# Stage passages of a two-block transformer kernel, taken tile by tile of the tokens

## The reference, cut to what matters

```python
x = x + 0.5 * g1 * swiglu(modulate(x, sh1, sc1), gate, up, down)   # FFN 1
x = x + g2 * token_mix(modulate(x, sh2, sc2), ...)                 # mix
x = x + 0.5 * g3 * swiglu(modulate(x, sh3, sc3), gate, up, down)   # FFN 2
# modulate(x, shift, scale) = rms_norm(x) * (1 + scale) + shift
# shift, scale, gate come from silu(c) @ w_ada + b_ada, for each stage anew
# swiglu(u) = (silu(u @ gate) * (u @ up)) @ down
# after two layers: x = rms_norm(x) * final_norm, then
# h = modulate_2(x, ...) enters the hybrid layer, h2 = modulate_2(x, ...) the experts
```

## Time and profile before

| | us |
|---|---|
| median of 3 runs (1957.5 to 1962.37) | 1959.36 |
| the profiled execution | 1957.13 |
| its span | 1955.5 |
| PE busy | 1812.3 (93%) |
| DVE busy | 1375.6 (70%) |
| ACT busy | 953.6 (49%) |
| DMA, mean over the span | 224 GB/s |
| chain that ended last | PE 77%, DVE 14%, ACT 4%, DMA 3%, issue 3% |
| mean granted TensorE clock | 0.956 |

### The profile page before, as it was taken

How to read it: one execution, slowest core, us unless ns; L and a number is a source line. 1 busy time by engine, 2 the same in 40 slices (tenths; PEclk the granted TensorE clock), 3 DMA queues, 4 the chain that set the end, 5 groups by cost and what they waited for, 6 DMA issues and landing times.

```text
span 1955.5 us, 25172 instructions
## 1 busy us (share of the span) xinstructions
PE 1812.3 (93%) x8756; PEld 1462.4 (75%) x8772; DVE 1375.6 (70%) x2086; ACT 953.6 (49%) x1427; POOL 47.1 (2%) x92
## 2 busy tenths in 40 slices
PE   6799999999999998999999989998997997999996
PEld 3688777777688767886878767886886675788875
DVE  6877755766766568776567567665677276999886
ACT  4344453654444443444446553444443245777774
POOL 0000000000000000000000000000000000000000
PEclk8899998999999999999989999999998598999998
DMA  9988741224766648884413347664685051999992
GB/s 368 348 307 306 281 144 65 108 92 150 259 252 246 248 174 322 321 306 174 144 65 108 108 173 290 243 244 178 232 326 217 0 193 67 354 352 368 352 352 112
DMA packets 61497, 437.41 MB, mean 224 GB/s; under 512 B 6768, under 2 KB 7280, under 8 KB 9200
## 3 DMA queue, kind: packets, MB, share of 16 engines
q1 hardware_dynamic: 47200, 339.27, 46.6%
q0 software_dynamic: 12672, 92.28, 12.8%
q10 hardware_dynamic: 1552, 4.89, 0.7%
HBM read 435.36 MB, written 1.05 MB: 223 GB/s over the span
## 4 chain that ended last, share of the span: by engine, by line
PE 77%; DVE 14%; ACT 4%; DMA 3%; issue 3%; POOL 0%; ACTq 0%; DVEq 0%; SPq 0%; POOLq 0%
PE bank L1609 22%; PE bank L1610 22%; PE bank L1611 22%; DVE w_lo L886 3%; DMA ada_w<-ada_pairs 2%; DVE ada_w L910 2%; PE bank L1819 2%; PE bank L1836 1%; PE bank L1689 1%; ACT w_hi L485 1%; PE bank L1797 1%; PE bank L1793 1%; PE bank L1799 1%; DVE arena L972 1%; DVE w_lo L893 1%
## 5 line engine op out<-in xcount | busy, mean ns | idle before, releaser
L886 DVE TENSOR_TENSOR w_lo<-raw,w_hi 128x1024 fp32r<-128x1024 f32 x428 | 504.0, 1221 | 258.1 <-ACT w_hi L485 257.1
L485 ACT ACTIVATE w_hi<-raw 128x1024 fp32r<-128x1024 f32 x428 | 428.7, 1053 | 419.1 <-PE bank L1611 413.9
L1609 PE MATMUL bank<-w_hi,uT_hi 128*128 128x512 f32 (+3 forms) x1440 | 561.2, 390 | 22.7 <-DVE uT_lo L1173 11.5
L1610 PE MATMUL bank<-w_lo,uT_hi 128*128 128x512 f32 (+3 forms) x1440 | 547.7, 380 | 0.0
L1611 PE MATMUL bank<-w_hi,uT_lo 128*128 128x512 f32 (+3 forms) x1440 | 546.1, 379 | 0.0
L1609 PEld LDWEIGHTS bank<-w_hi,uT_hi 128*128 128x128 f32 x1440 | 274.4, 191 | 81.6 <-DVE uT_lo L1173 13.5
L1609 PE MATMUL bank<-w_hi,r_arena 128*128 128x512 f32 (+1 forms) x744 | 301.8, 406 | 13.5 <-DVE r_arena L958 5.7
L1611 PEld LDWEIGHTS bank<-w_hi,uT_lo 128*128 128x128 f32 x1440 | 274.2, 190 | 52.0
L1610 PEld LDWEIGHTS bank<-w_lo,uT_hi 128*128 128x128 f32 x1440 | 274.9, 191 | 48.4 <-issue 1.4
L1611 PE MATMUL bank<-w_hi,r_arena 128*128 128x512 f32 (+1 forms) x744 | 297.6, 400 | 0.0
L1610 PE MATMUL bank<-w_lo,r_arena 128*128 128x512 f32 (+1 forms) x744 | 297.6, 400 | 0.0
(11 more groups left out here) (316 smaller groups left out, 1522.7 us busy)
## 6 DMA issues: line engine op xcount, KB each, us to landing
raw<-weight_stream SPq DMA_DIRECT2D x216, 1024.0 KB, 4.9
ada_w<-ada_pairs POOLq DMA_DIRECT2D x88, 1024.0 KB, 5.2
raw<-expert_blocks SPq DMA_DIRECT2D x48, 1024.0 KB, 4.8
ada_w<-expert_blocks SPq DMA_DIRECT2D x32, 1024.0 KB, 4.8
cmpw<-expert_blocks SPq DMA_DIRECT2D x16, 1024.0 KB, 4.8
arena<-ada_pairs SPq DMA_DIRECT2D x5, 1024.0 KB, 13.7
ada_w<-ada_pairs SPq DMA_DIRECT2D x3, 1024.0 KB, 13.2
cmpw<-compress_w ACTq DMA_DIRECT2D x2, 1024.0 KB, 8.3
```

The costliest lines, as they stand in the source:

```text
L485: act.activation(w_hi[:, b], v, ACT.Copy).then_inc(hi_done, 1)
L886: V.tensor_tensor(w_lo[:, b], v, f32(w_hi[:, b]), ALU.subtract).then_inc(split_done, 1)
L1609: pe.matmul(dst, xh, w_hi[:, off:off + n], start=first, stop=False, skip_group_check=True)
L1610: pe.matmul(dst, xh, w_lo[:, off:off + n], start=False, stop=False, skip_group_check=True)
```

## The change

In the code after, a passage is called `arrive` on each engine. x is updated in half rows (`update`), each followed by its own square on ACT (`square`), and the sum of two halves is made on DVE (`total`); ACT takes 1/D and EPS into the root. The normed row is made half on DVE and half on ACT. A tile is turned, scaled, rounded and subtracted in two halves of four k. Tile 1's updates stand between tile 0's steps in DVE's list. PE starts the next stage's first products with tile 0 and turns tile 1 at k = 6. The zero products before the turn are 10 in place of 16. The last FFN unit goes by tile: gate/up of tile 0, the gate product, `down` of the unit before, gate/up of tile 1 with the turn of tile 0 in its middle, then `last_down` by tile and half. The second unit's gate/up of tile 0 goes ahead of the first unit's turn. The first gate pair stands behind all splits of the first unit. On entry to FFN 2 the two rows of c are loaded behind the whole passage. The attention gates' products go in between tile 1's products of the mix. `LAST_UNIT` puts the last unit's third block ahead of the next stage's first.

```diff
-LAST_UNIT = (-1, 0, 3)
+LAST_UNIT = (-1, 0, 2)
 # ACT
-                norm(l * 3 + 2, l * 3 + 2, late=u_mix + MIX_IN_UNITS + MERGE_UNITS, c_row=l)
+            def arrive(q, n, blocks=lambda i: None):
+                square(q, 0)
+                normed(q, 0)
+                blocks(0)
+                act.wait_ge(mod_ready, n + 4)
+                turned(n, 0, 0)
+                blocks(1)
+                square(q, 1)
+                turned(n, 0, 1)
+                normed(q, 1)
+                for h in range(2):
+                    turned(n, 1, h)
...
+                arrive(l * 3 + 2, l * 3 + 2, lambda i: split(u_ffn, (i,)))
+                act.dma_start(c_bc, c_rows[0]).then_inc(c_landed, 16)
+                act.dma_start(c_next, c_rows[l]).then_inc(c_landed, 16)
+                act.wait_ge(c_landed, l * 32 + 48)
+                act.activation(c_bc, c_bc, ACT.Silu).then_inc(c_ready, 1)
+                act.activation(c_next, c_next, ACT.Silu).then_inc(c_ready, 1)
 # DVE
+            def arrive(stage, q, n, blocks=lambda i: None):
+                update(stage, 0, 0)
+                update(stage, 0, 1)
+                blocks(0)
+                total(q, 0)
+                normed(q, 0)
+                blocks(1)
+                dve.wait_ge(mod_ready, n + 4)
+                turned(n, 0, 0)
+                update(stage, 1, 0)
+                rest(n, 0, 0)
+                blocks(2)
+                turned(n, 0, 1)
+                update(stage, 1, 1)
+                rest(n, 0, 1)
+                total(q, 1)
+                normed(q, 1)
+                for h in range(2):
+                    turned(n, 1, h)
+                    rest(n, 1, h)
 # DVE, first unit of ffn2 (ffn1 alike, without the wait)
-                split(u0 + 1, (0,), LAST_BEHIND)
+                first_unit(u0, f0, stage)   # hidden 0, split, hidden 1, split, split
                 dve.wait_ge(c_ready, l * 2 + 3)
                 ada_pair(pair_place(l, "gate2", 0), mods_gate[:, 0:2])
-                hidden(f0)
-                split(u0 + 1, (1,), LAST_BEHIND)
-                split(u0, (2,), LAST_BEHIND)
                 h_split(f0)
 # PE
+            def arriving(n, q, more=lambda k, t: None):
+                def beside(k, t):
+                    if (k, t) == (0, 0):
+                        pe.wait_ge(x_ready, ...)      # tile 1's first half
+                    if (k, t) == (6, 0):
+                        turn_x(n, q, 1)
+                    if k % 4 == 0:
+                        pe.wait_ge(uT_ready, 4 * n + 2 * t + k // 4 + 1)
+                    more(k, t)
+                return beside
+            def arrive(n, q):
+                keep_warm(10, GU[0][:, :])
+                turn_x(n, q, 0)
...
+                pe.wait_ge(h_done, 2 * f0 + 1)
+                gate_up(u0 + 1, TILE[0])
+                turn(f0)
+                gate_up(u0 + 1, TILE[1])
```

More of the change, by code:

```diff
@@ L478, in _, with split @@
         def _(act):
-            def split(u, js, order=IN_LINE):
+            def split(u, js, order=IN_LINE, halves_=range(HALVES)):
                 for j in js:
@@ L508, in norm @@
[L508 to L529, removed]
@@ L533, in gate_out, with silu, h_tile @@
                 act.activation(gate_bc[:, h * 512:(h + 1) * 512], b[:, :], ACT.Copy).then_inc(gate_ready, 1)
[L535 to L539, removed]
+            def silu(u, f, tiles=range(T)):
+                for t in tiles:
+                    act.wait_ge(*((gu0_done, f + 1), (used[1], u + 2))[t])
+                    act.activation(act_g[:, t], GU[t][:, 0:F_UNIT], ACT.Silu).then_inc(silu_done, 1)
+            def h_tile(f, t, psum, done):
+                s = slice(t * P, (t + 1) * P)
+                act.wait_ge(*psum)
+                act.activation(hT_hi[:, :, s], HT[:, :].rearrange("p (f s) -> p f s", f=2)[:, :, s], ACT.Copy).then_inc(done, 1)
             def h_split(f):
@@ L951, in hidden, with turned, rest @@
-            def hidden(f):
-                for t in range(T):
+            def turned(n, t, h):
+                s = slice(t * P, (t + 1) * P)
+                dve.wait_ge(uT_psum, 4 * n + 2 * t + 2)
+                for i in range(2):
+                    c = 4 * h + 2 + i
+                    e = V.tensor_scalar(uTf[:, c, s], turned_banks(n)[t][1][:, (2 * h + i) * P:(2 * h + i + 1) * P], modf[:, 8 + c:9 + c], modf[:, c:c + 1], ALU.mult, ALU.add)
+                e.then_inc(uTf_done_v, 1)
+            def rest(n, t, h):
+                s = slice(t * P, (t + 1) * P)
+                dve.wait_ge(uT_hi_done, 4 * n + 2 * t + h + 1)
+                V.tensor_tensor(uT_lo[:, 4 * h:4 * h + 4, s], uTf[:, 4 * h:4 * h + 4, s], f32(uT_hi[:, 4 * h:4 * h + 4, s]),
+                                ALU.subtract).then_inc(uT_ready, 1)
@@ L1000, in ffn1 @@
                     h_split(f0 + i)
-                split(u0 + n, (0,), LAST_BEHIND)
+                for j in range(2):
+                    ada_pair(pair_place(l, "end1", j), mods[:, 36 + 2 * j:38 + 2 * j])
                 dve.wait_ge(mods_kept, l * 17 + 10)
@@ L1044, in ffn2, with merge @@
                     h_split(f0 + i)
-                split(u0 + n, (0,), LAST_BEHIND)
                 dve.wait_ge(mods_kept, l * 17 + 18)
                 modulation(stage + 1, mods[:, 40:56], gain=vec[:, bass.ds(V_GAIN + l * 8, 8)])
-                split(u0 + n - 1, (2,), LAST_UNIT)
-                hidden(f0 + n - 1)
-                h_split(f0 + n - 1)
-                split(u0 + n, (1,))
-                x_update(stage, (used[2], u0 + n + 1))
-            def merge(u0, m, stage, gates, following, between, more=True):
+                last_unit(u0, f0 + n - 1, n)
+            def merge(u0, m, gates, following):
                 split(u0, (2,))
@@ L1081, in merge @@
                 split(u0 + 2, (2,))
-                x_update(stage, (used[1], u0 + 4), between=between)
-                if more:
-                    split(u0 + 3, (0,))
             def job_bias(j0, jobs, j):
@@ L1725, in ffn @@
-                turn(f0 + n - 1)
-                down(u0 + n - 1, f0 + n - 1, last=True)
+                turn(f - 1)
+                gate_up(u0 + n - 1, TILE[0])
+                pe.wait_ge(gate_ready, 2 * nn + 1)
+                gate(nn, 1, SPARE)
+                down(u0 + n - 2, f - 1)
+                gate_up(u0 + n - 1, TILE[1], beside=lambda k, t: turn_tile(f, 0, hL_psum) if k == KD // 2 else None)
+                last_down(u0 + n - 1, f)
             def half_product(lhs, chunks, closes, ready, done, late=lambda: None):
```

446 lines of the change are left out of this document (260 added, 186 removed).

## The result

| | before | after |
|---|---|---|
| median us (4 runs each) | 1958.43 | 1995.84 |
| lowest to highest | 1955.44 to 1962.37 | 1992.45 to 1999.15 |
| the profiled execution | 1957.13 | 1992.45 |
| its span | 1955.5 | 1990.8 |
| mean granted TensorE clock | 0.956 | 0.939 |

The account below looks back on a forecast made before the run. PE, busy 93%, with its gaps bounded by a DVE, ACT, PE, DVE chain, DVE's list and pair loads. The terms, mainly +14.6 (mix to FFN 2) and +6.4 (experts' entry), summed to +24.5 us on 1957.13, hence 1982; range 1957 to 1994.

Parts of the forecast that it names:

- steps 1, 3, 5: FFN 1 to mix (+1.4, +1.0 us), FFN 2 to FFN 1 (-1.2), FFN 2 to the hybrid layer (-3.2).
- E: Time mark: the start of a stage's last gate/up product.
- step 3: FFN 2 to FFN 1: gate/up ends earlier, but PE waits for the pair chain at the second turn; -1.2 us.
- step 6: Hybrid merge to the experts: tile 1's update waits for tile 0's turn, gate copy later; +6.4 us, bounds +3 to +8.
- Step 2: Mix to FFN 2, twice: late c rows and DVE's list delay the second turn; +7.3 us each, +14.6.
- The real price is in DVE's list: Mix to FFN 2: the first gate pair, behind DVE's three splits, makes the second turn +5.5 us later.
- L: Time mark: the end of a merge's last product.
- a later wait takes such a loss in: Half-pace losses after new waits in mix to FFN 2, FFN 2 to FFN 1, first FFN 1: absorbed, no term.
- The clock: Half-rate products behind waits: +2.6 us in FFN 1 to mix and the hybrid entry, +1.8 per mix to FFN 2.
- A: Faster: DVE's list does not decide, second unit's hidden ready when PE ends down; 1943 us, chance 0.13.
- B: No change: waits at k = 4 mostly absent, experts' entry costs 3, pair chain 4 us sooner; 1960 us, chance 0.09.
- C: Worse: passages restart at 1.2 GHz at k = 4 and tile 1, c's rows land after 7.0 us; 1992, chance 0.14.

Follow-up runs that it names:

- x6: Kernel after, at the experts' entry only: tile 1's half updates on DVE and squares on ACT moved ahead of tile 0's scaling; 1987.45 us, ratio 1.0145.
- b2: Kernel before, with only the first gate pair of each FFN moved behind all splits of the first unit in DVE's list; 1959.48 us, ratio 1.0012.
- x5: Kernel after, with the four pairs of each FFN's own gate no longer all ahead of the second unit's hidden in DVE's list; 1962.75 us, ratio 1.0033.
- b1: Kernel before, with only the four gate pairs of each FFN spread over units 1 to 3 behind the hidden tiles; 1949.02 us, ratio 0.9945.
- w1: Kernel after, with zero products in the waits of passages, first units, second turns and mixes; 1984.30 us, ratio 1.0139.
- x4: Kernel after, with tile 1's squares moved behind the scaling and rounding of tile 0's second half in ACT's list; 1977.21 us, ratio 1.0107.
- w2: Kernel before, with zero products ahead of FFN turns, the hybrid layer's norms and in the mixes' waits; 1950.71 us, ratio 0.9960.
- y3: A faster kernel with zeros in the passages and reordered loops, plus 8 more zero products in each of two mix waits; 1910.96 us, ratio 0.9769.

## Why the prediction was right in sign and wrong in size

- **The passages themselves** (steps 1, 3, 5): right, order and times, to 0.2 us at four points of FFN 1 to mix; FFN 2 to FFN 1 reached gate/up's end at E+28.7 (28.4), the hybrid layer's first block ended at E+40.3 (39.1). But the waits of 2.8 and 2.0 us at k = 4 were 1.06 and 0.28: the places were right while part of the waits was filled by slow products.
- **Given back at the second turn** (step 3): right. Up to there FFN 2 to FFN 1 was 6.4 us ahead, and this wait took 4.8 back (it was 6.19). PE after:

```profile
757.44 1.11 PE L1798 MATMUL bank<-cst,arena 128*128 128x128 f32 x4 [11.74 <-DVE arena L1024]
```

- **The experts' entry** (step 6): +7.3 for +6.4, and x6 shows its cause.
- **Step 2 failed in size**, +22.5 (x6: +21.1) for +14.6, that is 7.9 us; with 5.5 us inside the mixes, for which the sum had no term, less 2.4 us by which the other places together came out lower, this is the miss of about 11 us in span. Three things in it. (a) "The real price is in DVE's list", with the first pair's place as its cause and 5.5 us each: moving that place alone costs 2.6 and 1.8 in its profile and nothing that the medians show (b2), because an earlier first turn pays for a later second one, and that gain was not in the step. The list is the price, but by its length: pairs, reloads, gate, split and hidden follow the end of the passage as one chain, and x5, which takes it out of the way, brings 13 of the 22.5 us back where b1 brings none. (b) The list began 1.9 us later than reckoned: the products between k = 4 and tile 1's turn ran at half pace, so gate/up ended at L+25.0 and not 23.4 (in w1's second layer, all at full pace, it ended at L+23.5), and ACT had c's silu done at L+26.7 and not 24.4. The pairs' reloads added 0.8. (The wait at the second turn is 4.81 and 5.11 us and not 6.4, since PE itself came there later.) (c) The booking "a later wait takes such a loss in" holds only for a wait whose end is fixed by other work. The second turn's is not, since its chain starts where the passage ends. In the second layer the second unit began at half pace too, the first turn came later for it, and pairs 1 and 3 with it; with half pace filled away (w1) the second turn stood at L+53.0 in place of L+56.3, and the passage cost 5.2 us less. In the first layer the zeros gained nothing (L+54.1 for 53.8). PE after (L is 1165.20), then w1 (1157.27):

```profile
1195.40 0.77 PE L1697 MATMUL bank<-w_hi,uT_hi 128*128 128x512 f32 x1 [4.42 <-DVE w_lo L932]
...
1221.51 1.11 PE L1798 MATMUL bank<-cst,arena 128*128 128x128 f32 x4 [5.11 <-DVE arena L1024]
```

```profile
1210.25 0.66 PE L1801 MATMUL bank<-cst,arena 128*128 128x128 f32 x4 [2.56 <-DVE arena L1024]
```

In this second layer of w1 no stretch of products on the way ran at half pace, and its second turn still comes 1.9 us behind the forecast's L+51.1: that part is not the clock.

- **The clock**: +6.2 in all was forecast (2.6, and 1.8 twice). Summed over all products by which their pitch (start to start) exceeds that at full pace, half pace took 13 to 19 us more after than before, by how the products next to a wait are counted; some of it lies ahead of waits, where it is free. The inside of the mixes, for which the sum had no term, gave 5.5.
- **Rivals.** A needed `hidden` not to stand behind the pairs; it did, and x5 shows what that is worth, 33 us. B is out: the experts' entry cost 7.3 and not 3, and of the 17.4 us of waits at k = 4 that it wanted mostly absent 7.6 us were there (2.59 and 2.64 in mix to FFN 2); in the passages to mix and to FFN 2 the rest was filled by products at half pace and not saved by cheaper scalings, since k = 4 came when it was forecast. C lies nearest, 1992, by its price, and that is luck in part: half pace behind the waits was there as it says, but c's rows landed after 4 us, not 7, and with the clock filled in both kernels the change still costs 34 of 37 us.
- The range ended 2 us above C and had no term for the inside of the mixes, nor for a list that begins later and is longer than reckoned.

Still open: how much of the +22.5 is clock in the mean over executions (single ones of one kernel lay up to 20 us apart), what makes up the 9.3 us that mix to FFN 2 costs with the pairs spread, and why x4's median gained 18.6 where its profile accounts for 10.4.

## What to carry to other kernels

Before a change makes a stream start earlier, look for the next wait whose releaser hangs on a list that starts with the same event: there the gain goes, and that list is to be spread first (here 9 us in the old kernel, about three times that in the new one, by the places of a few instructions). When a passage is taken in halves, each engine's list has to be ordered by who waits, square, update and scaling alike; here one line in the wrong order made a third to a half of the loss. And a clock that falls in waits is a term for all stages, also for those that the change does not touch.

## What the hardware showed that I had not expected

- The clock can fall in the midst of products and not at their restart: after 2.87 us of standing PE ran at full pace from 251.30 and at half pace from 252.66 on. After the same wait of 2.87 us it was at half pace at once at 495.34. So the prediction's "every resumption behind a long wait starts low" does not hold here.
- Behind waits of 1.7 us it was low in some profiled executions and not in others, with the same list around them: 32 small products took 3.76 to 6.5 us. With the waits filled (w1, w2, y3) they took 3.76 in all six places.
- Zeros in such waits and the longer ones brought both kernels something, 11.5 and 7.6 us in the medians, though they compute nothing.
